# Modulation items of 1024 columns, and a projection that starts on the lower half of the features

## The chip, the core and the metric

One core of a Trainium2 chip runs the whole program. The metric is the device time of one execution in microseconds, as the median of several runs. TensorE (PE) does the matrix products, VectorE (DVE) and ScalarE (ACT) the elementwise work, GpSimd (POOL) and SyncE (SP) mostly issue DMAs; every engine works through its own instructions in order and is held back by semaphores. Numbers are fp32. A weight tile is therefore split into a high part (`whi`) and a low part (`wlo`), and a product is made of three matmuls: high by high, high by low, low by high.

## The reference

Two blocks of two layers each, for 256 tokens of width 1024. Only the first block is touched. Each of its four sub-layers is a "sandwich" that is modulated by a vector `c`:

```
def modulation(c, w, b):
    return jnp.split(jax.nn.silu(c) @ w + b, 3, axis=-1)

def sandwich(x, mod, g_pre, g_post, fn):
    shift, scale, gate = mod
    h = rms_norm(x, g_pre) * (1.0 + scale[:, None]) + shift[:, None]
    return x + gate[:, None] * rms_norm(fn(h), g_post)
```

`w` is a matrix of 1024 rows and 3072 columns (12 MB), one for each sub-layer: shift, scale and gate, 1024 columns each. The sub-layers are: 0, a hybrid mixer (`h @ hyb_w_in`, then pooling over windows and a gated recurrence, then `@ hyb_w_out`); 1, a feed-forward; 2, a dilated attention (`h @ att_w_qkv`); 3, a feed-forward.

## The kernel before

**Modulation.** `silu(c) @ w` is a product of one row with a big matrix. VectorE computes it as sums over the 8 groups of 128 rows: an *item* multiplies a tile of 128 rows by 512 columns with a column of `sc` (silu(c)) and adds it to an accumulator `acc_a` (or `acc_b`). TensorE then adds up the 128 partitions with a matmul against ones. Sub-layer 0 needs its shift and scale first of all: 4 column blocks x 8 items, loaded as 8 loads of 1 MB each into the six slots of `raw`, the buffer that the weights use too (`load`, line 378; `ada_first`, line 1325). Five of the 32 items are done by TensorE directly on the loaded rows (`DIRECT`, line 335; `ada_cols`, line 2512). `add_cols` (line 2499) does the sums and `mod_cols` (line 1346) makes the shift and scale columns from them, at its end `scol` at line 1351. Only then can the features of the normed x be shifted and scaled (`pre`, line 647 on ScalarE and 1507 on VectorE).

All other modulation (gate of sub-layer 0, then sub-layers 1 to 3) goes through `ada_ring`, two slots of 1 MB, each with 4 tiles of 128 x 512. GpSimd issues a load when VectorE has finished the 4 items of the slot (`ada_blocks`, line 455; semaphore `ada_step`). The items (`ada_item`, line 1302) are woven by hand into VectorE's order: behind the first blocks of the projection, into the eight levels of the recurrence, into the first feed-forward, and behind each block of four splits in the qkv projection (line 1799).

**Start.** SyncE loads the first four modulation loads, then x, four more, and then the projection's weights, two loads per column block (features 0 to 511 and 512 to 1023). ScalarE copies small tables, squares x for the norm, makes `xn1`, and after the modulation columns walks over the 8 feature groups: shifted h as fp32 and as high part, with the first weight splits between them. Then it issues the loads of `masks`, `bandqk` (pooling bands) and `poolw` (lines 809 to 811). TensorE turns x, does the column sums with `warm_ones` between them, and then projects block after block (`proj`, line 2254): all four half tiles of block 0 (kind A: tokens on partitions, matmuls of 512), then all four of block 1 (kind B, matmuls of 256). Behind them it waits for all three tables (`band_in`, line 2547) and multiplies the bands, then block 2, and then eight half blocks with the scores of one level of the recurrence after each (`level_scores`, line 2558), which wait for VectorE's `level` and `merge` (lines 1735 and 1724). VectorE's product at line 1719 starts the levels.

A split needs its tile of `raw`, and its slot among four in `whi`/`wlo` to be free: the high part by ScalarE (line 542), then the low one by VectorE (line 1299).

Of the kernel before, what the change touches and what calls it, by code (L numbers as in the profile page):

```python
# [24 lines left out]
P = 128  # L25
# [63 lines left out]
def program(nc, t):  # L89

    with ExitStack() as ctx:
# [27 lines left out]
        with ExitStack() as first:  # L119
            ada_ring = sb(first, "ada_ring", [P, 2, 4, 512])  # L120
# [165 lines left out]

        def slot(n):

            return (n + ADA_FIRST) % RAW

        def in_count(n):

            return 16 * ((n + ADA_FIRST) // RAW + 1)
# [41 lines left out]
        DIRECT = {6: (3,), 7: (2, 3)}  # L335
        DVE_LAST, PE_LAST = (4, 5), (6, 7)
# [40 lines left out]
        def _(sp):  # L377
            def load(n, it, src):
# [4 lines left out]
                if n >= RAW:  # L383
                    sp.wait_ge(s["lo_ready"], 2 * (n - RAW) + 2 + 12 * it)
                elif n + ADA_FIRST >= RAW:
                    sp.wait_ge(s["ada_used"], n + ADA_FIRST - RAW + 1)
                    if n + ADA_FIRST - RAW in DIRECT:
                        sp.wait_ge(s["ada_pe"], n + ADA_FIRST - RAW - 5)
                dst = raw[:, slot(n), :].rearrange("p (k n) -> p k n", k=k)
                sp.dma_start(dst, ap).then_inc(raw_in[slot(n)], 16)  # L390
# [63 lines left out]
        def _(pool):  # L454
            def ada_blocks(first, blocks):

                for i, (j, n) in enumerate(blocks):
                    b = first + i
                    for kh in range(2):
                        if b:  # L460
                            pool.wait_ge(s["ada_step"], 8 * (b - 1) + 4 * (kh + 1))
                        src, _ = src_cols(t["ada_w"][j // 2, j % 2], n, kh)
                        pool.dma_start(ada_ring[:, kh, :, :], src).then_inc(ada_in[kh], 16)  # L463
# [21 lines left out]
            SHIFT_SCALE, GATE = [0, 512, 1024, 1536], [2048, 2560]  # L485
            pool.wait_ge(s["ada_used"], ADA_FIRST)
            ada_blocks(0, [(0, n) for n in GATE])
            gain_row(0)
            ada_blocks(2, [(1, n) for n in SHIFT_SCALE])
            ada_blocks(6, [(1, GATE[0])])  # L490
            gain_row(1)
            ada_blocks(7, [(1, GATE[1])] + [(2, n) for n in SHIFT_SCALE + GATE])
# [5 lines left out]
            ada_blocks(14, [(3, SHIFT_SCALE[0])])  # L498
            gain_row(3)
            ada_blocks(15, [(3, n) for n in SHIFT_SCALE[1:] + GATE])  # L500
# [29 lines left out]
        def _(act):  # L530
# [116 lines left out]
            def pre(j):  # L647

                if j < 4:
                    act.wait_ge(s["mod_ready"], j + 1)  # L650
                for k in range(KD):
                    if j < 4 and k % 2:
                        act.wait_ge(s["h32_ready"], 4 * j + k // 2 + 1)
# [129 lines left out]

            for g in range(3):
                act.wait_ge(s["vec_dil"], g + 1)
                A.activation(vrow[:, g * VLEN_DIL:(g + 1) * VLEN_DIL], ps[0:8, 4 + g, 0:VLEN_DIL], ACT.Copy,
                             scale=1.0 / DIL_SCALE).then_inc(s["vec_dil_c"], 1)
            act.wait_ge(s["vec_dil"], 4)
            A.copy(vrow[:, 3 * VLEN_DIL:], ps[0:8, 7, :]).then_inc(s["vec_dil_c"], 1)
# [5 lines left out]
            norms(0)  # L795
            act.wait_ge(s["root_x"], 1)
            act.wait_ge(s["ssq_x"], 2)
            A.activation(xn1[:, 0, :], x[:, 0, :], ACT.Copy, scale=small[:, 5, 3:4]).then_inc(s["xn_ready"], 1)
            act.wait_ge(s["const_in"], 48)
            act.wait_ge(s["root_x"], 2)  # L800
            A.activation(diag[:, :], ident[:, :], ACT.Copy, scale=small[:, 5, 4:5]).then_inc(s["diag_ready"], 1)
            split(0)
            pre(0)
# [9 lines left out]
            for b in range(3):  # L813
                proj("hyb_in", HYB[b:b + 1], f1, tok1, b)
# [468 lines left out]
        def _(dve):  # L1283
# [18 lines left out]
            def ada_item(acc, b, n, k, it=0, bias=None):  # L1302

                kh, kk = k // 4, k % 4
                if kk == 0:
                    dve.wait_ge(ada_in[kh], 16 * (b + 1) + 32 * it)
                out = acc[:, bass.ds(n, 512)]
                if k == 0 and bias is not None:
                    dve.wait_ge(s[f"wrow_in{bias}"], 16)
                    ins = V.scalar_tensor_tensor(out=out, in0=ada_ring[:, kh, kk, :], scalar=sc[:, k:k + 1],  # L1310
                                                 in1=gg[:, bias, n:n + 512], op0=ALU.mult, op1=ALU.add)
                elif k == 0:
                    ins = V.tensor_scalar(out, ada_ring[:, kh, kk, :], sc[:, k:k + 1], None, ALU.mult)
                else:
                    dve.wait_ge(s["ada_step"], 8 * b + k + 16 * it)
                    ins = V.scalar_tensor_tensor(out=out, in0=ada_ring[:, kh, kk, :], scalar=sc[:, k:k + 1],  # L1316
                                                 in1=out, op0=ALU.mult, op1=ALU.add)
                ins.then_inc(s["ada_step"], 1)

            def ada_part(acc, b, n, kh, it=0, bias=None):  # L1320
# [1871 lines left out]
```

## Time and profile before

| what | us |
|---|---|
| median of 3 runs | 1269.61 (1267.96 to 1271.66) |
| the profiled execution | 1269.97 |
| its span | 1268.2 |
| TensorE, busy | 1248.5 |
| VectorE, busy | 933.9 |
| ScalarE, busy | 718.2 |

The profile is one execution. Its page names the busy time of each engine, the chain of work that ended last, and the costliest groups of instructions. From the trace come the chain in order of time, the instructions of an engine in a stretch, who waited for whom, the DMA issues with their time to landing, and stretches with the granted TensorE clock. A matmul that is written once in fp32 without a split shows as two. Matmul ends are modelled, so the busy share of TensorE says little; waits before an instruction and the distance between starts say more.

### The profile page before, as it was taken

The page shows a single profiled execution, that of the slowest core. Times are in us where ns is not written, and L with a number is a line of the kernel's source. Part 1 is how long each engine was busy: PE and PEld are TensorE (multiplying, and loading weights), DVE is VectorE, ACT ScalarE, POOL GpSimd, SP SyncE. Part 2 cuts the span into 40 slices and gives each one's busy share as a digit, 9 for nine tenths or more (in the row PEclk, how much of TensorE's full clock was granted, in tenths as well). Part 3 has the DMA queues.
Part 4 walks back from the last instruction along what each step waited for, and adds up shares of the span by engine and source line. Part 5 has one row for each costly group of instructions (what it writes and reads, how often), then busy time and mean ns, then how long its engine had stood idle before and what let it go on. Part 6 is the DMA issues. An engine that isn't in the chain of part 4 may idle for free.

```text
span 1268.2 us, 20841 instructions
## 1 busy us (share of the span) xinstructions
PE 1248.5 (98%) x8024; PEld 1133.6 (89%) x8024; DVE 933.9 (74%) x1222; ACT 718.2 (57%) x1069; POOL 50.8 (4%) x76
## 2 busy tenths in 40 slices
PE   8999999999999999999999999999999999999999
PEld 6998899999999778999989989888888888888888
DVE  6889988886899658666676695676666677666665
ACT  3676754444744557444467764665555667655554
POOL 1101000000111000000001000000000000000000
PEclk8999999999999999999999999999999999999999
DMA  9986989996799734666556544356565542366650
GB/s 348 372 297 208 339 290 325 334 327 205 244 361 370 230 67 153 206 203 200 199 166 211 162 150 155 132 198 200 200 202 202 190 163 95 122 220 204 202 166 34
DMA packets 147248, 274.41 MB, mean 216 GB/s; under 512 B 4759, under 2 KB 85679, under 8 KB 147048
## 3 DMA queue, kind: packets, MB, share of 16 engines
q1 hardware_dynamic: 132320, 220.21, 51.5%
q0 software_dynamic: 13616, 50.94, 11.9%
q10 hardware_dynamic: 1240, 2.26, 0.5%
q8 instruction: 49, 0.80, 0.3%
q14 instruction: 23, 0.19, 0.0%
HBM read 272.30 MB, written 1.10 MB: 216 GB/s over the span
## 4 chain that ended last, share of the span: by engine, by line
PE 82%; DVE 8%; DMA 4%; ACT 3%; issue 2%; ACTq 0%; POOL 0%; DVEq 0%; POOLq 0%
PE ps L2229 80%; DMA ada_ring<-in_ada_w 4%; DVE wlo L1299 2%; DVE acc_a L1316 2%; ACT whi L542 1%; PE ps L2682 1%; DMA voh<-in_voh 1%; ACT xn L603 0%; PE ps L2416 0%; PE ps L2399 0%; DVE rs L1949 0%; ACT h L659 0%; DVE prob L1906 0%; ACT hboth L654 0%; PE ps L2976 0%
## 5 line engine op out<-in xcount | busy, mean ns | idle before, releaser
L1299 DVE TENSOR_TENSOR wlo<-raw,whi 128x1024 fp32r<-128x1024 f32 x400 | 483.5, 1222 | 222.8 <-ACT whi L542 222.0
L542 ACT CAST whi<-raw 128x1024 fp32r<-128x1024 f32 x400 | 416.6, 1048 | 404.0 <-PE ps L2229 389.6
L2229 PE MATMUL ps<-hboth,whi 128*128 128x256 f32 (+1 forms) x2720 | 605.2, 311 | 1.0 <-DVE hboth L1529 0.5
L2229 PE MATMUL ps<-hboth,wlo 128*128 128x256 f32 x1792 | 491.6, 274 | 0.7 <-DVE hboth L1524 0.4
L2229 PEld LDWEIGHTS ps<-hboth,whi 128*128 128x128 f32 x2720 | 447.2, 191 | 30.1 <-issue 6.2
L2229 PEld LDWEIGHTS ps<-hboth,wlo 128*128 128x128 f32 x1792 | 343.9, 192 | 3.1 <-issue 0.6
L2229 PE MATMUL ps<-whi,hidhi 128*128 128x512 f32 x434 | 164.5, 379 | 0.0
L2229 PE MATMUL ps<-wlo,hidhi 128*128 128x512 f32 x434 | 164.1, 378 | 0.0
L2229 PE MATMUL ps<-whi,hidlo 128*128 128x512 f32 x434 | 164.1, 378 | 0.0
L2229 PE MATMUL ps<-whi,hboth 128*128 128x512 f32 (+1 forms) x512 | 155.8, 375 | 3.0 <-DVE wlo L1299 0.9
L2229 PEld LDWEIGHTS ps<-whi,hboth 128*128 128x128 f32 x512 | 95.5, 190 | 18.5 <-issue 5.1
L1316 DVE SCALAR_TENSOR_TENSOR acc_a<-ada_ring,sc,acc_a 128x512 f32<-128x512 f32 (+1 forms) x124 | 93.1, 751 | 7.6 <-DMA ada_ring<-in_ada_w 3.7
L2229 PE MATMUL ps<-wlo,hboth 128*128 128x512 f32 (+1 forms) x256 | 93.8, 366 | 0.0
L2229 PEld LDWEIGHTS ps<-whi,hidlo 128*128 128x128 f32 x434 | 82.0, 189 | 11.5
L2229 PEld LDWEIGHTS ps<-wlo,hidhi 128*128 128x128 f32 x434 | 82.1, 189 | 11.4 <-issue 0.2
L2229 PEld LDWEIGHTS ps<-whi,hidhi 128*128 128x128 f32 x434 | 82.2, 189 | 10.5 <-ACT whi L542 0.2
L2229 PEld LDWEIGHTS ps<-wlo,hboth 128*128 128x128 f32 x256 | 48.7, 190 | 6.2 <-issue 1.0
L463 POOL DMA_DIRECT2D ada_ring<-in_ada_w x40 | 30.0, 751 | 296.0 <-DVE acc_a L1316 212.6
L1651 DVE TENSOR_REDUCE tmp<-ps 128x512 f32<-128x1024 f32 x32 | 38.9, 1217 | 3.5 <-PE ps L2229 3.5
L1656 DVE TENSOR_TENSOR hidlo<-hid,hidhi 128x512 fp32r<-128x512 f32 x32 | 22.1, 692 | 16.6 <-ACT hidhi L760 16.6
L603 ACT ACTIVATE xn<-x 128x512 f32<-128x512 f32 (+1 forms) x32 | 19.3, 602 | 10.7 <-DVE x L1418 5.7
L755 ACT ACTIVATE tmp<-tmp 128x512 f32<-128x512 f32 x32 | 20.1, 627 | 2.9 <-DVE tmp L1651 2.9
(259 smaller groups left out, 1118.6 us busy)
## 6 DMA issues: line engine op xcount, KB each, us to landing
raw<-in_ffn_w_in SPq DMA_DIRECT2D x44, 1024.0 KB, 7.2
ada_ring<-in_ada_w POOLq DMA_DIRECT2D x40, 1024.0 KB, 7.9
raw<-in_w_mlp_up SPq DMA_DIRECT2D x32, 1024.0 KB, 5.4
raw<-in_w_mlp_down SPq DMA_DIRECT2D x32, 1024.0 KB, 4.9
raw<-in_ffn_w_out SPq DMA_DIRECT2D x22, 1024.0 KB, 5.1
raw<-in_att_w_qkv SPq DMA_DIRECT2D x18, 1024.0 KB, 7.3
raw<-in_w_in_even SPq DMA_DIRECT2D x18, 1024.0 KB, 5.1
raw<-in_hyb_w_in SPq DMA_DIRECT2D x10, 1024.0 KB, 11.2
```

The lines of the kernel that those rows point to most:

```text
L463: pool.dma_start(ada_ring[:, kh, :, :], src).then_inc(ada_in[kh], 16)
L542: A.copy(whi[:, H % 4, :], raw[:, slot(n), h * HALF:(h + 1) * HALF]).then_inc(s["hi_ready"], 1)
L603: A.activation(xn_of(j)[0][:, i // 2, c], x[:, i // 2, c], ACT.Square, accum_out=stat[:, 4 + i:5 + i]).then_inc(s["ssq_x"], 1)
L755: A.activation(tmp2[:, g % 3, :], tmp2[:, g % 3, :], ACT.Relu).then_inc(s["mrelu"], 1)
L1299: V.tensor_tensor(wlo[:, H % 4, :], raw[:, slot(n), h * HALF:(h + 1) * HALF], whi[:, H % 4, :].bitcast(F32), ALU.subtract).then_inc(s["lo_ ...
L1316: ins = V.scalar_tensor_tensor(out=out, in0=ada_ring[:, kh, kk, :], scalar=sc[:, k:k + 1], in1=out, op0=ALU.mult, op1=ALU.add)
L1651: V.tensor_reduce(in_order(tmp2[:, g % 3, :], 2), parts_of(UP_BANK[g % 3]), AX, ALU.add) \
L1656: V.tensor_tensor(hidlo2[:, g % 3, :], hid2[:, g % 3, :], hidhi2[:, g % 3, :].bitcast(F32), ALU.subtract).then_inc(s["mhid_lo"], 1)
L2229: return pe.matmul(out, lhsT, rhs, start=first, stop=last, skip_group_check=True)
L2682: m = pe.transpose(dl_turned(p, i)[:, (j - j0) * P:(j - j0 + 1) * P], dl_block(p, j), ident[:, :])
```

## The change

1. Ring items are 1024 columns wide: `ada_ring` holds 2 slots of 2 tiles of 128 x 1024. A load brings 256 rows of one part (shift, scale or gate) and is freed after two items. Bytes and multiplications are the same, items half as many. In the scale of sub-layer 1, TensorE's direct share becomes one group of rows (7) of 1024 columns instead of two of 512.
2. The order of the weaving follows: one wide item in each of the levels 1 to 7, two per stretch in the feed-forward, and in the qkv stage one item behind each split.
3. Sub-layer 0's first shift and scale: the loads come in the order lower half of shift, lower half of scale, upper half of shift, upper half of scale (`ADA_COLUMNS`); x is the second load; the lower weight halves of blocks 0 and 1 are loaded before the upper modulation loads. `first_mod(half)` makes the columns of 4 feature groups at a time. Two more items go to TensorE (`DIRECT`, load 3).
4. TensorE runs the lower halves of both blocks (q 0 to 3), then the sums for the upper features, then the upper halves (q 4 to 7). x is turned by transposes of both token tiles. The warming matmuls are 32 at the start, 12 and 8 later, and none between the halves. ScalarE does the first norm before it copies the tables of the bias, and issues the band tables behind the work of the upper features.

```diff
-            ada_ring = sb(first, "ada_ring", [P, 2, 4, 512])
+            ada_ring = sb(first, "ada_ring", [P, 2, 2, D])
...
-        DIRECT = {6: (3,), 7: (2, 3)}
-        DVE_LAST, PE_LAST = (4, 5), (6, 7)
+        ADA_COLUMNS = (0, 1024, 512, 1536)
+        DIRECT = {3: (2, 3), 6: (3,), 7: (2, 3)}
+        PE_LAST = 7
...
-            for a in range(ADA_FIRST):
-                load(a - ADA_FIRST, 0, src_cols(t["ada_w"][0, 0], (a // 2) * 512, a % 2))
-                if a == 3:
-                    sp.dma_start(x[:, :, :], t["x"][0].rearrange("(t p) n -> p t n", p=P)).then_inc(s["x_in"], 16)
-            proj(FIRST["hyb_in"], t["hyb_w_in"][0], HYB)
+            load_ada(0)
+            sp.dma_start(x[:, :, :], t["x"][0].rearrange("(t p) n -> p t n", p=P)).then_inc(s["x_in"], 16)
+            for a in range(1, 4):
+                load_ada(a)
+            for n in range(2):
+                load(n, 0, src_cols(t["hyb_w_in"][0], HYB[n][1], 0))
+            for a in range(4, ADA_FIRST):
+                load_ada(a)
+            for n in range(2, 4):
+                load(n, 0, src_cols(t["hyb_w_in"][0], HYB[n - 2][1], 1))
+            proj(FIRST["hyb_in"] + 4, t["hyb_w_in"][0], HYB[2:])
...
-            def ada_blocks(first, blocks):
...
+            def ada_loads(first, rows):
+
+                for i, (j, n, q) in enumerate(rows):
+                    l = first + i
+                    if l >= 2:
+                        pool.wait_ge(s["ada_step"], 2 * (l - 1))
+                    src, _ = src_down(t["ada_w"][j // 2, j % 2][:, n:n + D], 2 * P * q)
+                    pool.dma_start(ada_ring[:, l % 2, :, :], src).then_inc(ada_in[l % 2], 16)
...
+            act.wait_ge(s["turned"], 8)
+            for half in range(2):
+                split(4 * half)
+                act.wait_ge(s["mod_ready"], half + 1)
+                first_pre((4 * half, 4 * half + 1))
+                split(4 * half + 1)
+                first_pre((4 * half + 2, 4 * half + 3))
+                split(4 * half + 2)
+                split(4 * half + 3)
...
-            for a in range(4):
-                ada_first(a)
+            ada_first(0)
             mean_x(0, 0)
             mean_x(0, 1)
-            for a in range(4, ADA_FIRST):
+            for a in range(1, 4):
                 ada_first(a)
-            mod_cols(0, 0)
+            first_mod(0)
             split(0)
-            pre(0)
+            first_low(0)
+            first_low(1)
+            split(1)
+            first_low(2)
+            ada_first(4, (0,))
+            first_low(3)
+            split(2)
+            ada_first(4, (1, 2, 3))
+            split(3)
+            for a in range(5, ADA_FIRST):
+                ada_first(a)
+            first_mod(1)
+            split(4)
...
-                for q in range(i, i + 1) if i < 6 else range(3 * i - 12, 3 * i - 9):
-                    b, k = (q + 20) // 8, (q + 20) % 8
-                    ada_item(acc_a, b, 512 * b, k)
...
+                if 1 <= i <= 6:
+                    ada_item(acc_a, 1, D, i + 1)
...
             for b in range(8):
-                proj("qkv", (QKV_B * 2 + QKV_A)[b:b + 1], b)
-                if b < 6:
-                    ada_block(acc_a, 14 + b, 512 * b)
+                for q in range(4):
+                    split(2 * (FIRST["qkv"] + 2 * b) + 4 + q)
+                    if b < 6:
+                        ada_item(acc_a, 7 + b // 2, D * (b // 2), 4 * (b % 2) + q)
...
-            proj("hyb_in", HYB[0:2], j=0)
+            for q in range(8):
+                b = q // 2 % 2
+                proj_half(HYB[b][0], 2 * b, q, 2 * (q // 4) + q % 2, 0, None if b else 0)
+                if q == 3:
+                    add_cols(2)
+                    ada_cols(6)
+                    ada_cols(7)
+                    add_cols(3)
             pe.wait_ge(s["proj_free"], 1)
             pe.wait_ge(s["band_in"], 48)
```

## Rows read from the trace of the kernel before

**Rows 1.** The page's engine table: busy us, share, instructions.
```profile
PE 1248.5 (98%) x8024; PEld 1133.6 (89%) x8024; DVE 933.9 (74%) x1222; ACT 718.2 (57%) x1069; POOL 50.8 (4%) x76
```
**Rows 2.** The chain that ended last, by time: start us, us, what.
```profile
67.61 8.65 DMA ada_ring<-in_ada_w
...
81.33 1.22 DVE bandqk L1719
...
156.98 175.93 PE ps L2229 x1310
```
**Rows 3.** Waits of TensorE, 38 to 116 us: total, times, longest.
```profile
PE ps L2229 <- issue: 0.8, 1, 0.8
```
**Rows 4.** VectorE's instructions by time: start us, us, what, idle before.
```profile
11.12 3.11 DVE L1335 SCALAR_TENSOR_TENSOR acc_a<-raw,sc,acc_a 128x512 f32<-128x512 f32 x4 [1.92 <-DMA raw<-in_ada_w]
...
21.72 0.15 DVE L1394 TENSOR_SCALAR small<-stat 128x1 f32<-128x1 f32 x1 [1.27 <-ACT xn L603]
...
28.43 3.17 DVE L1335 SCALAR_TENSOR_TENSOR acc_a<-raw,sc,acc_a 128x512 f32<-128x512 f32 x4
...
35.84 0.17 DVE L1351 SCALAR_TENSOR_TENSOR scol<-scol,cols 128x8 f32<-128x8 f32 x1
36.04 1.22 DVE L1299 TENSOR_TENSOR wlo<-raw,whi 128x1024 fp32r<-128x1024 f32 x1
...
37.63 0.41 DVE L1524 TENSOR_TENSOR hboth<-h,hboth 128x256 fp32r<-128x256 f32 x1
```
**Rows 5.** ScalarE's instructions by time; ACTq are its DMA issues.
```profile
19.03 0.63 ACT L603 ACTIVATE xn<-x 128x512 f32<-128x512 f32 x1 [2.80 <-DMA x<-in_x]
...
39.01 0.56 ACT L659 ACTIVATE h<-ps,shcol,scol 128x256 f32<-128x256 f32 x1
...
43.45 0.36 ACTq L809 DMA_DIRECT2D masks<-in_masks  x1
...
44.82 0.46 ACTq L811 DMA_DIRECT2D poolw<-in_pool_w  x1
```
**Rows 6.** Stretches: length, busy us by engine, granted clock, DMA share, GB/s.
```profile
18.00:19.00 1.00, 1.00 (x8) 1.00 (x7) 0.96 (x2) 0.00 (x0) 0.00 (x0) 0.69 1.03 385
...
36.00:37.00 1.00, 1.00 (x6) 1.00 (x6) 0.97 (x2) 0.96 (x2) 0.00 (x0) 0.50 1.09 408
...
30.00:40.00 10.00, 10.00 (x71) 9.80 (x72) 5.57 (x11) 4.32 (x8) 1.54 (x2) 0.83 1.05 388
```
**Rows 7.** DMA issues, 43 to 45.5 us: KB each, us to landing.
```profile
bandqk<-in_band ACTq DMA_DIRECT2D x1, 1024.0 KB, 8.5
...
masks<-in_masks ACTq DMA_DIRECT2D x1, 512.0 KB, 4.5
poolw<-in_pool_w ACTq DMA_DIRECT2D x1, 256.0 KB, 11.3
```
**Rows 8.** TensorE's instructions by time.
```profile
9.91 5.71 PE L2229 MATMUL ps<-voh,vtab 33*8 33x384 f32 x8 [3.99 <-DMA voh<-in_voh]
...
34.50 0.95 PE L2229 MATMUL ps<-ones,acc_a 128*128 128x1 f32 x8
...
38.39 0.77 PE L2229 MATMUL ps<-whi,hboth 128*128 128x512 f32 x1
...
59.90 3.62 PE L2229 MATMUL ps<-bandqk,tok 128*128 128x256 f32 x16
```
**Rows 9.** VectorE in the levels of the recurrence, by time.
```profile
88.89 0.73 DVE L1316 SCALAR_TENSOR_TENSOR acc_a<-ada_ring,sc,acc_a 128x512 f32<-128x512 f32 x1
89.55 0.77 DVE L1747 TENSOR_TENSOR bandqk<-pooled,tot 128x512 f32<-128x512 f32 x1
...
113.31 0.16 DVE L1749 TENSOR_TENSOR tot<-f 128x8 f32<-128x8 f32 x1
```
**Rows 10.** Waits of ScalarE, 160 to 330 us; its copy in the qkv stage.
```profile
ACT whi L542 <- PE ps L2229: 86.5, 61, 1.6
...
402.08 1.01 ACT L550 COPY f<-ps 128x1024 f32 x1
```

More of the change, by code:

```diff
@@ L793, in _, with first_pre @@
             act.dma_start(t["vec_swa"], vrow[:, 3 * VLEN_DIL:]).then_inc(s["vec_out"], 16)
[L795 to L802, printed above, removed]
-            pre(0)
+            def first_pre(parts):
+                for k in parts:
+                    if k >= 4:
+                        act.wait_ge(s["hlo_ready"], k - 3)
+                    A.activation(h32_slot(0, k), turned_ps(0, k), ACT.Identity, bias=shcol[:, 0, k:k + 1],
+                                 scale=scol[:, 0, k:k + 1])
+                    A.activation(hhi[:, k, :], turned_ps(0, k), ACT.Identity, bias=shcol[:, 0, k:k + 1],
+                                 scale=scol[:, 0, k:k + 1]).then_inc(s["hhi_ready"], 1)
+            act.wait_ge(s["turned"], 8)
[7 more added lines that the diff above has]
+                split(4 * half + 3)
             act.wait_ge(s["lb_step"], 1)
@@ L813, in _ @@
             for b in range(3):
-                proj("hyb_in", HYB[b:b + 1], f1, tok1, b)
+                if b == 0:
+                    split(8)
+                    split(9)
+                    evac(0, 6, "A", HYB[0][2], f1, tok1)
+                elif b == 1:
+                    split(10)
+                    split(11)
+                    evac(1, 8, "B", HYB[1][2], f1, tok1)
+                else:
+                    proj("hyb_in", HYB[b:b + 1], f1, tok1, b)
                 if b == 1:
@@ L1308, in ada_item @@
                 if k == 0 and bias is not None:
                     dve.wait_ge(s[f"wrow_in{bias}"], 16)
[L1310 to L1311 removed]
+                    ins = V.scalar_tensor_tensor(out=out, in0=row, scalar=sc[:, k:k + 1], in1=gg[:, bias, :],
+                                                 op0=ALU.mult, op1=ALU.add)
@@ L1318, in ada_item, with ada_items @@
+                    ins = V.scalar_tensor_tensor(out=out, in0=row, scalar=sc[:, k:k + 1], in1=out, op0=ALU.mult,
+                                                 op1=ALU.add)
                 ins.then_inc(s["ada_step"], 1)
-            def ada_part(acc, b, n, kh, it=0, bias=None):
-                for kk in range(4):
-                    ada_item(acc, b, n, 4 * kh + kk, it, bias)
-            def ada_first(a):
-                dve.wait_ge(raw_in[a % RAW], 16 * (a // RAW + 1))
+            def ada_items(acc, w, n, ks, it=0, bias=None):
+                for k in ks:
+                    ada_item(acc, w, n, k, it, bias)
@@ L1328, in ada_first @@
+            def ada_first(a, parts=range(4)):
+                at = ada_ring_at(a)
+                dve.wait_ge(raw_in[at % RAW], 16 * (at // RAW + 1))
                 mine = [kk for kk in range(4) if kk not in ada_direct(a)]
-                for kk in mine:
-                    k, w = 4 * (a % 2) + kk, raw[:, a % RAW, kk * 512:(kk + 1) * 512]
+                for kk in [kk for kk in mine if kk in parts]:
+                    k, w = 4 * (a % 2) + kk, raw[:, at % RAW, kk * 512:(kk + 1) * 512]
                     out = acc_a[:, (a // 2) * 512:(a // 2 + 1) * 512]
@@ L1353, in mod_cols, with first_mod, first_low @@
                     .then_inc(s["mod_ready"], 1)
-                dve.wait_ge(s["mod_ready"], j + 1)
+                dve.wait_ge(s["mod_ready"], j + 2)
+            def first_mod(half):
+                k, bank = 4 * half, 4 * half
+                dve.wait_ge(s["cols_sum"], 2 * half + 2)
+                V.tensor_tensor(shcol[:, 0, k:k + 4], ps[:, bank, 0:4], col("b_shift", k, 4), ALU.add)
+                link(V.tensor_tensor(scol[:, 0, k:k + 4], ps[:, bank, 4:8], col("b_scale", k, 4), ALU.add))
+                V.scalar_tensor_tensor(out=scol[:, 0, k:k + 4], in0=scol[:, 0, k:k + 4], scalar=1.0,
+                                       in1=col("g_pre", k, 4), op0=ALU.add, op1=ALU.mult) \
+                    .then_inc(s["mod_ready"], 1)
+            def first_low(k):
+                dve.wait_ge(s["hhi_ready"], k + 1)
+                V.tensor_tensor(hlo[:, k, :], h32_slot(0, k), hhi[:, k, :].bitcast(F32), ALU.subtract) \
+                    .then_inc(s["hlo_ready"], 1)
             def gate_add(j, bank):
```

192 lines of the change are left out of this document (106 added, 86 removed).

## The prediction

> **What bounds the kernel now.** I read the page's engine table first, then the chain of waits from its start, then the waits of TensorE, and only then single stretches. TensorE is busy for 98% of the span [rows 1], so there is little to win except where it starts late or waits. The chain says where that is. Until 49 us it runs through TensorE only in name: from 26 to 38 us the engine does sums of a few columns and warming matmuls, and the first matmul of the projection is at 38.39 [rows 8]. Between 50 and 93 us the chain is not TensorE's: it goes through the modulation items on VectorE and the loads of their ring (8.65 us for one) up to the product at L1719 [rows 2]. Yet TensorE itself waits hardly at all there: after 38.4 us its longest wait is 0.8 us, at 112.7 [rows 3]. So two legs run side by side from 38 to 113 us within one microsecond of each other: TensorE's matmuls, and VectorE with its ring. Whoever shortens one gets only what the other allows. From 157 us the chain is TensorE alone for 176 us at a stretch [rows 2].
>
> The first 38 us have three limits. DMA moves 388 GB/s or so without a pause [rows 6], 2.7 us for a load of 1.05 MB. VectorE needs 0.785 us for each item (3.17 us for four, with the wait between them) and ends its last one at 31.6; the modulation columns are done at 36.04 [rows 4]. TensorE can't start before them.
>
> **Early phase, lower features.** x is moved from fifth to second load. The first load lands at 6.3 as before; x takes the place of the second, which VectorE used at 11.12, so x is there at 11.1. VectorE's second mean comes 2.7 us after ScalarE's first square (19.03 and 21.72, [rows 4, 5]), so at 13.9, and the weights of load 1, now third, are there at that time too. Load 1: 3.15 us, load 2: 2.85, two items of load 3: 1.6; VectorE is at 21.5. TensorE turns x and takes two rows of load 3 itself; its column sums take 1 us (0.95, [rows 8]) and the three small operations 0.5: lower columns at about 23.2. Their two halves of each block run from about 25 to 36.5.
>
> **Upper features.** After 23.2 VectorE has 4 weight splits (1.14 apart, 4.6), 4 low parts (0.4 each, 1.6 [rows 4]), 13 items (9.9) and about 1.5 us of waits for ScalarE: 40.8. Sums and columns again 1.5: the upper columns are ready at 42.3, against 36.0 now for all of them. That is the price of the split order: the same column work, with 4 splits and 4 low parts now ahead of it. ScalarE is the queue for what follows (for each feature row two shifted copies, 0.56 long and 0.46 apart [rows 5], and a split of 0.95 for every second). First upper matmul at 43.9. The eight half blocks take 59.90 - 38.39 = 21.5 us [rows 8], so four take 10.75: 54.7. I add 0.5 for ScalarE and 1.0 for the clock: 56.2, against 59.9. The matmuls of the lower halves lie under VectorE's 13 items, so they cost nothing; if they ran late the upper ones would follow them.
>
> The clock: between the lower and the upper halves the new TensorE order holds column sums and waits, and the warming matmuls are gone. In the trace the granted clock fell to 0.50 at 36 us after such columns although the engine counted as busy, and in the other place, after 4 us without matmuls (5.9 to 9.9), it came back to 1.00 only within the microsecond from 18 to 19 [rows 6, 8]. So the upper halves will start at the lower of the two levels (1.2 GHz); from the first place, about 3 us of it, half lost and part of that beside ScalarE, 1.0 us; from the second, 8.8 us of it, 4.4 us. The Trainium skill (TensorE: Matmul & The Clock Gate, "Why this matters for your kernels") advises against gaps between bursts of matmuls, which speaks against this order; by it TensorE would be ready at 59.6 at worst, and the trace agrees that the engine falls back.
>
> **The tables behind it.** The wait that I expect to be last is a hidden one. After these blocks TensorE multiplies the pooling bands at 59.90 and needs masks, bands and pool weights. ScalarE issues them in program order behind the copies of the last features: at 43.45 to 44.82, 7.4 us after the columns, and they landed at 56.1, 12.7 us from the first issue (masks 4.5, bands 8.5, pool weights 11.3) [rows 5, 7]. That left 3.8 us of slack. In the new order ScalarE has all copies and splits of the upper half ahead of them; with the same three instructions of lead over the engine I get 4.3 us after the columns: 46.6. Landing: if the queue got an even half of 385 GB/s, its 1.84 MB take 9.6 us (56.2); as in the trace 12.7 (59.3); and up to 3.1 us more (62.4) when the third ring load, issued near 53.9 now, shares with the pool weights, which are short rows. I take 60.3, nearest to the trace, plus 1 for the ring load. So TensorE, ready at 56.2, multiplies the bands at 60.3: 0.4 later than now. The cover that made ScalarE's place free is gone.
>
> **TensorE's leg.** From the bands to the end of the level scores it goes from 59.90 to 112.7, of which 0.8 was waiting [rows 2, 3]: 111.9 if nothing is late, plus 0.4: 112.3.
>
> **VectorE's leg.** An item of 1024 columns isn't in the trace. Below: a split of the same size, 1.22 us, 1.14 apart [rows 4]; above: two items of 512, 1.57 chained or 1.32 among other work (0.66 each, 88.89 to 89.55 [rows 9]). I take 1.3 chained and 1.2 among other work, near the split, since both read two inputs of 1024. Up to the product 20 old items (15.7) become 10 (13.0): 2.7 less. They start at 51.2 instead of 51.60. Ring loads carry the same bytes and are freed after two items as after four before. The product can't come before ScalarE's and TensorE's part, though: bands at 60.3, copy at 64, eight small operations, four splits, evacuation and Silu near 78. I get its end at 79.3 by ScalarE and at 80.9 by the ring, 80.1 in the middle, instead of 82.5 (81.33 + 1.22, [rows 2]). Then the levels: six single items (0.66, one of them cheaper) and three more at 109.81 (2.3), 6.0 in all, become six items of 1.2, 7.2 in all. So 31.0 us from the product to the last level step (113.3 to 113.5 [rows 9]) become 32.2. Leg: 80.1 + 32.2 = 112.3, against 113.5. The item that stood ahead of the low part (L1764) is gone (0.66), but TensorE waits for ScalarE's copy beside it, so I count nothing.
>
> **Afterwards.** From 115.5 to 148 TensorE has no wait, and its column sums hold as many matmuls as before (8 direct ones on one row of 1024 instead of two of 512). In the first feed-forward ScalarE waits for TensorE 61 times, 86.5 us [rows 10]: VectorE's savings there are worth nothing. In the qkv stage the blocks follow at 10.72 us, and only the one evacuated at 402.08 [rows 10] came 0.34 later than that, since splits stood behind eight items and a ring load. Interleaved, a ring slot needs two items, a split and a load (3.6, and 8 as for the loads of the start), 11.6 us against 10.72, about 4 us over five blocks, but each split now has some 6 us of room and no longer four splits behind eight items. I count 0.3 gained; the loss of that cover would cost up to 4.
>
> **Sum.** Legs 112.3 against 113.5: 1.2, and 0.3: 1.5 us. Profiled execution 1269.97 (span 1268.2 and 1.8 around it) - 1.5 = 1268.5; it stands 0.4 above the median of 1269.61.
>
> **Rivals.** (B) The tables are in time (56.2) and the product at 78: TensorE's leg 108.2, VectorE's 110.2, gain 3.3 + 0.3: 1266.4; with upper columns at 40.5 instead of 42.3, some 5.5: 1264.5. For it: the DMA may have idle room near 45 us, as loads wait for slots then. Against: ScalarE's order, and VectorE's levels, which get longer. (C) Slower: the tables, at the bands' matmul. It decides from 61.5 on, where TensorE's leg passes 113.5; at 63.5 it costs 2.0 less 0.3: 1271.7, and only past 65.3 more than 0.3%. The slow clock (59.6) delays the ring's freeing and adds to it. (D) The wide items save nothing (1.32 among other work, 1.57 chained): product 2.7 later, 82.8, levels 0.7 more: leg 115.7, 1271.9. (E) The change doesn't do what it says in the qkv stage: the ring falls behind, splits are late, up to 3 us: 1271.5.
>
> **How the numbers follow.** Forecast 0.50, B 0.27, C 0.13, D 0.05, E 0.05. About 0.3% (3.8 us) is what a measurement can tell from no change. More than that is reached by the far part of B (0.18) and by the far part of C with D or E on top (0.10); within it: 0.72. Range: 1264.3 takes in B's far end, 1272.4 takes in C at 64.
>
> **What would show it.** Upper columns (L1351's successor) at 42.3 and the first upper matmul at 43.9; a wait of TensorE of about 4 us for the pool weights ahead of the band matmul; items of 1024 at 1.28 us busy; the last level step at 112.3; the first feed-forward unchanged in length. Wrong would be: no wait at the bands, level steps paced by TensorE, or a gap in qkv.

## The result and the profile after

The changed kernel is slower by 0.17%: 1272.55 us against 1270.16, medians of 20 runs each, a ratio of 1.0017 with the interval 1.0009 to 1.0025. Its profiled execution has a span of 1271.4 us against 1268.2. TensorE is as busy as before and VectorE 20 us less [rows 1]; the page's first line of busy times:

```profile
PE 1249.7 (98%) x8012; PEld 1137.8 (89%) x8012; DVE 913.8 (72%) x1140; ACT 721.5 (57%) x1073; POOL 48.9 (4%) x76
```

So the loss isn't work, it is waiting. The chain that ended last, by time (start us, us, what), says where; it answers to [rows 2]:

```profile
65.73 8.99 DMA ada_ring<-in_ada_w
...
113.74 32.65 PE ps L2318 x178
...
155.02 175.93 PE ps L2318 x1310
...
376.97 7.97 DMA ada_ring<-in_ada_w
384.94 0.02 issue
384.96 1.28 DVE acc_a L1374
386.25 1.14 DVE wlo L1357
387.38 1.21 DVE acc_a L1374
388.59 0.29 issue
388.88 9.55 DMA ada_ring<-in_ada_w
398.43 0.02 issue
398.45 1.28 DVE acc_a L1374
```

The long piece of the first feed-forward starts at 155.02 instead of 156.98 and is as long as before, 175.93. Up to 332 us the changed kernel is 1.96 us ahead in this pair of profiles (how far single profiles can be trusted for that is said in the last section). Then, from 352 to 401, the chain no longer holds TensorE at all: it goes round through an item of the ring, a split, the slot's second item, the issue and the next load. ScalarE's copies close the blocks; of before (two lines, the second one is the last copy of the stage) and of after (three):

```profile
391.02 1.01 ACT L550 COPY f<-ps 128x1024 f32 x1
...
437.46 1.01 ACT L552 COPY tok<-ps 128x1024 f32<-128x1024 f32 x1
```
```profile
391.44 1.01 ACT L584 COPY f<-ps 128x1024 f32 x1
406.47 1.01 ACT L584 COPY f<-ps 128x1024 f32 x1
...
440.68 1.01 ACT L586 COPY tok<-ps 128x1024 f32<-128x1024 f32 x1
```

These blocks are 10.72 us apart when nothing is late. After's copies at 391.44 and 406.47 are 15.0 apart; before's at 391.02 and 402.08 [rows 10] 11.1. The lead of 1.96 has turned into a lag of 3.2 at 440, and nothing changes behind that. The 50 us from 350 to 400 (length, busy us by engine, granted clock, DMA share, GB/s), before and then after:

```profile
350.00:400.00 50.00, 49.89 (x447) 49.73 (x446) 46.99 (x56) 23.44 (x23) 7.03 (x10) 1.00 1.02 372
```
```profile
350.00:400.00 50.00, 46.57 (x413) 46.06 (x412) 36.73 (x33) 22.53 (x22) 5.62 (x8) 1.00 0.98 349
```

One number is useful for all that follows: from the start of the long feed-forward piece to the last of these copies it is 437.46 - 156.98 = 280.48 us before and 440.68 - 155.02 = 285.66 after. I call it the stretch F. The time from the start of the program to that piece I call S.

### The profile page after: what moved, and what is told of

Same layout as the page of the kernel before. It is cut to its first block, busy times and chain, and to the rows that moved or that the text cites. A ratio compares the mean times of both kernels' runs of the same rounds, so it can differ in the third digit from the quotient of the medians.

```text
span 1271.4 us, 20717 instructions
## 1 busy us (share of the span) xinstructions
PE 1249.7 (98%) x8012; PEld 1137.8 (89%) x8012; DVE 913.8 (72%) x1140; ACT 721.5 (57%) x1073; POOL 48.9 (4%) x76
## 4 chain that ended last, share of the span: by engine, by line
PE 80%; DVE 8%; DMA 5%; ACT 4%; issue 3%; ACTq 0%; SPq 0%; DVEq 0%
PE ps L2318 78%; DMA ada_ring<-in_ada_w 4%; DVE wlo L1357 2%; DVE acc_a L1374 2%; ACT whi L576 1%; DMA x<-in_x 1%; PE ps L2780 1%; ACT xn L637 1%; PE ps L2505 0%; DVE rs L2038 0%; ACT h L693 0%; DVE prob L1995 0%; DVE acc_a L1394 0%; PE ps L2488 0%; ACT hboth L688 0%
## 5 line engine op out<-in xcount | busy, mean ns | idle before, releaser
L2318 PEld LDWEIGHTS ps<-wlo,hidhi 128*128 128x128 f32 x434 | 82.3, 190 | 11.3 <-issue 0.2
L2318 PEld LDWEIGHTS ps<-whi,hidlo 128*128 128x128 f32 x434 | 82.3, 190 | 11.3
L1374 DVE SCALAR_TENSOR_TENSOR acc_a<-ada_ring,sc,acc_a 128x1024 f32<-128x1024 f32 (+1 forms) x62 | 79.5, 1282 | 14.0 <-DMA ada_ring<-in_ada_w 13.1
```

Source lines behind the costliest of these rows:

```text
L1374: ins = V.scalar_tensor_tensor(out=out, in0=row, scalar=sc[:, k:k + 1], in1=out, op0=ALU.mult, op1=ALU.add)
L2318: return pe.matmul(out, lhsT, rhs, start=first, stop=last, skip_group_check=True)
```

## The experiments

**Order or width in the qkv stage.** Two things are new there: an item stands behind each split, and items are twice as wide. Four kernels take these apart, and the start with them. The first is the changed kernel with its items grouped as before:

```diff
             for b in range(8):
-                for q in range(4):
-                    split(2 * (FIRST["qkv"] + 2 * b) + 4 + q)
-                    if b < 6:
-                        ada_item(acc_a, 7 + b // 2, D * (b // 2), 4 * (b % 2) + q)
+                proj("qkv", (QKV_B * 2 + QKV_A)[b:b + 1], b)
+                if b < 6:
+                    for q in range(4):
+                        ada_item(acc_a, 7 + b // 2, D * (b // 2), 4 * (b % 2) + q)
```

> The changed kernel, with its four wide items of a qkv block behind the block's four splits again instead of one behind each split. Theory S (how long a ring slot is held): interleaved, the two items of a slot have a split between them, so a slot is held 3.6 us and then needs a load of 8 to 9.5 us, 11.6 to 13.1 against a block of 10.72; grouped it is held 2.6 us, so 10.6 plus. The ring keeps up, the 1.96 us won before the qkv stage stay, the copy that is at 406.47 in the changed kernel is at 400 to 401, and the time is 1270.2 - 2.0 = 1268.2 (1267.7 to 1268.9). Rival W (the load itself became slower because its rows are 1024 columns long, 8 to 9.5 us instead of 7.3 to 8.3): the ring stays late in either order, 1270.5 to 1272.5.

Measured: 1265.89 us, 0.9965 of before (0.9952 to 0.9977), 6.7 less than the changed kernel; it is the fastest of all. Rival W falls. F is 278.97 us. The forecast of 1268.2 was too high by 2.3, because I took before to be free of this loss; it isn't (run e8_before_light). VectorE's order in one block, by time:

```profile
357.10 2.60 DVE L1374 SCALAR_TENSOR_TENSOR acc_a<-ada_ring,sc,acc_a 128x1024 f32<-128x1024 f32 x2
360.67 2.60 DVE L1374 SCALAR_TENSOR_TENSOR acc_a<-ada_ring,sc,acc_a 128x1024 f32<-128x1024 f32 x2 [0.97 <-DMA ada_ring<-in_ada_w]
363.19 4.62 DVE L1357 TENSOR_TENSOR wlo<-raw,whi 128x1024 fp32r<-128x1024 f32 x4
```

And its stretch from 350 to 400:

```profile
350.00:400.00 50.00, 50.00 (x439) 49.68 (x438) 43.72 (x38) 23.81 (x24) 7.83 (x11) 1.00 1.03 392
```

VectorE still waits for the ring (0.97), but it does so when the block's splits are done, and TensorE has no gap in 50 us.

The second is the kernel before with narrow items interleaved:

```diff
             for b in range(8):
-                proj("qkv", (QKV_B * 2 + QKV_A)[b:b + 1], b)
-                if b < 6:
-                    ada_block(acc_a, 14 + b, 512 * b)
+                for q in range(4):
+                    split(2 * (FIRST["qkv"] + 2 * b) + 4 + q)
+                    if b < 6:
+                        ada_item(acc_a, 14 + b, 512 * b, 2 * q)
+                        ada_item(acc_a, 14 + b, 512 * b, 2 * q + 1)
```

> The kernel before, with its items of 512 columns, but in the qkv stage two of them behind each split instead of eight behind the four splits. Theory S: a slot's four items have a split in their middle, so it is held 4 x 0.785 + 1.14 = 4.3 us and with a load of 8 its cycle is 12.3 us against 10.72: as in the changed kernel VectorE waits for the ring with splits behind the wait, and about 5 us are lost in the qkv stage: 1273 to 1276. Rival W (width is the cause): no loss, 1270.2 within 0.5.

Measured: 1276.00 us, 1.0046 of before (1.0029 to 1.0063), as theory S has it. F is 286.81. The order costs about as much with narrow items: 6.2 us by the medians, but against a kernel that loses some itself (run e8_before_light); against an F without loss, 278.96, it is 7.9 here and 6.7 with wide items.

The third weaves the wide items in pairs:

```diff
                 for q in range(4):
                     split(2 * (FIRST["qkv"] + 2 * b) + 4 + q)
-                    if b < 6:
-                        ada_item(acc_a, 7 + b // 2, D * (b // 2), 4 * (b % 2) + q)
+                    if b < 6 and q % 2:
+                        ada_items(acc_a, 7 + b // 2, D * (b // 2), (4 * (b % 2) + q - 1, 4 * (b % 2) + q))
```

> The changed kernel with its qkv items woven in another way: two items behind every second split instead of one behind each. Two splits still stand behind each pair of items, but the two items of a ring slot are next to each other, so a slot is held 2.6 us as with grouped items, not 3.6. Theory S (the time a slot is held counts): the cycle is 2.6 + 8 = 10.6 us, the ring keeps up: 1265.9 (1265.4 to 1266.9). Rival O (splits that stand behind an item's wait for a load are what costs, however long a slot is held): half of the 6.7 us and more stays: 1269 to 1272.5.

Measured: 1266.48 us, 0.9970 of before (0.9960 to 0.9980). F is 279.09. The 6 us are gone, although two splits still stand behind each pair, and rival O falls. The loads are no faster; us to landing of the ring's ten loads from 345 to 405 us (min, median, max), in the changed kernel and then in this one:

```profile
DMA to landing us min/median/max: 7.1/8.4/9.6
```
```profile
DMA to landing us min/median/max: 6.8/8.4/9.5
```

So what costs is the split between the two items of one slot: it makes the slot be held longer.

The fourth leaves the order alone and takes away bytes:

```diff
+                    width = D // 2 if l >= 30 else D
-                    src, _ = src_down(t["ada_w"][j // 2, j % 2][:, n:n + D], 2 * P * q)
-                    pool.dma_start(ada_ring[:, l % 2, :, :], src).then_inc(ada_in[l % 2], 16)
+                    src, _ = src_down(t["ada_w"][j // 2, j % 2][:, n:n + width], 2 * P * q)
+                    pool.dma_start(ada_ring[:, l % 2, :, 0:width], src).then_inc(ada_in[l % 2], 16)
```

> The changed kernel, interleaved in the qkv stage as it is, but the last ten ring loads bring only 512 of their 1024 columns (the other half of an item multiplies what lay in the slot, so the shift, scale and gate of sub-layer 3 are not computed). All instructions, waits and orders stay. Theory S (a slot's load arrives after its item is due): with half the bytes a load takes 4 to 5 us instead of 8 to 9.5, the cycle is 8 to 9 us against 10.72, the gap vanishes: 1265.9, as with grouped items. Rival O (the order itself delays the splits, since VectorE has an item ahead of each): no or little change, 1271 to 1272.5.

Measured: 1266.27 us, 0.9975 of before (0.9966 to 0.9985). F is 278.96. Rival O falls here too. A load of half the bytes still took 6.7 us to land, not the 4 to 5 that I gave it, against 8.4 in the changed kernel; 1.7 us less per load was enough. (The weights' loads got more room as well, so this run alone would not prove the held slot; the pairs above, with all bytes, do.)

**The start and the width, each alone.** The start alone, with the items, the loads of the ring and all later orders of before:

```diff
-            ada_ring = sb(first, "ada_ring", [P, 2, 2, D])
+            ada_ring = sb(first, "ada_ring", [P, 2, 4, 512])
...
-            ada_items(acc_a, 0, 0, range(4), 0, 0)
+            ada_block(acc_a, 0, 0, 0)
             proj("hyb_in", HYB[1:2], 1)
-            ada_items(acc_a, 0, 0, range(4, 8))
+            ada_block(acc_a, 1, 512, 0)
```

> The kernel before with the new start alone (loads of the lower columns first, lower halves of two blocks ahead of the upper columns, ScalarE's new order), ring items of 512 columns and all later orders as before. Theory of two legs: TensorE reaches the bands 1.8 us earlier (58.1 instead of 59.90), but VectorE's items and their ring still end at about 82 before the product and 113.1 at the last level step, so only about 0.4 us reach the end: 1269.8 (1269.2 to 1270.3). Rival P (TensorE's start alone decides): the whole 1.8: 1268.4.

Measured: 1269.83 us, 0.9999 of before (0.9989 to 1.0008). F is 281.96, 1.5 us worse than before's. The forecast was met in its number only, and this run alone can't tell whether a gain at the start was lost again. The two runs with light loads, below, take that up.

The wide items alone, with the start of before and grouped in the qkv stage:

```diff
-            ada_ring = sb(first, "ada_ring", [P, 2, 4, 512])
+            ada_ring = sb(first, "ada_ring", [P, 2, 2, D])
...
-                    ada_block(acc_a, 14 + b, 512 * b)
+                    for q in range(4):
+                        ada_item(acc_a, 7 + b // 2, D * (b // 2), 4 * (b % 2) + q)
```

> The kernel before with ring items of 1024 columns alone, grouped behind the splits in the qkv stage, and the old start. Theory of two legs: VectorE's ten wide items ahead of the product take 2.7 us less, but TensorE's own work from the bands (59.90) to the end of the level scores held only 0.8 to 1.6 us of waits, so the end of the levels comes 0.5 to 1.2 earlier: 1269.0 to 1269.7. Rival V (VectorE's leg alone decides): 1.8 earlier as in the changed kernel: 1268.4.

Measured: 1267.42 us, 0.9979 of before (0.9969 to 0.9989), with F at 278.96, 1.5 shorter than before's. Against before it hit neither number, since the qkv part of the gain was in neither theory.

So both sides need a qkv stage that can't lose. The kernel before and the start alone, with half the bytes in the last ring loads (the same edit for both):

```diff
+                        width = 256 if b >= 15 else 512
-                        pool.dma_start(ada_ring[:, kh, :, :], src).then_inc(ada_in[kh], 16)
+                        pool.dma_start(ada_ring[:, kh, :, 0:width], src[:, :, 0:width]).then_inc(ada_in[kh], 16)
```

> The kernel before with its last ten ring loads reduced to half their bytes (shift, scale and gate of sub-layer 3 not computed), the rest unchanged. In its qkv stage one block came 0.34 us late and one 1.18 us late. Theory S: both are the ring's, so 1.5 us vanish: 1268.3 (1267.5 to 1268.9). Rival: they are of another cause, no change: 1269.8.

> The new start alone on ring items of 512 columns (run e3_start_only), with the last ten ring loads reduced to half their bytes (shift, scale and gate of sub-layer 3 not computed), so that the qkv stage can lose nothing to the ring. Against run e8_before_light it shows what the start alone is worth. Theory of two legs: VectorE's narrow items and their ring hold the levels, 0.4 us less than e8_before_light (0 to 0.7). Rival P: the start's own 1.5 to 1.8 us, which in run e3_start_only were lost again in the qkv stage.

Measured: 1267.04 us (0.9981; 0.9972 to 0.9990) for before and 1268.27 (0.9990; 0.9982 to 0.9999) for the start alone; F is 278.96 in both. The kernel before thus loses 1.5 us to the ring in its profile, and some 2.5 by the medians (1269.52 in that series, 1267.04); the forecast of 1267.5 to 1268.9, made from the profile, was too high. The start alone, which rival P put 1.5 to 1.8 us ahead and my theory 0.4, gains nothing; it came out 1.2 behind. Four kernels without a loss in the qkv stage (F 278.96 or 278.97), medians:

| | start of before | new start |
|---|---|---|
| items of 512 | 1267.04 | 1268.27 |
| items of 1024 | 1267.42 | 1265.89 |

Each part alone is worth nothing or less; the two together are worth 1.15 us. Only the rows were measured in one series each: there the new start is 1.2 slower with narrow items and 1.5 faster with wide ones. The 1.15 goes across series; with each kernel against its own before it is 1.5 (3.9 less against 2.5 less), and it is not much more than the noise. That the start pays only with wide items fits two legs of nearly the same length. The columns mix two ways to spare the qkv stage, but run e6_half_bytes, wide items and new start with light loads, is at 1266.27, so that the way matters little. Whether the start costs anything without wide items isn't settled: the two legs don't explain it, the intervals of the upper two overlap, the run times of one kernel spread by 1 to 4 us, and in their profiles the last level step is at the same time. First the band matmul on TensorE and that step on VectorE before (light):

```profile
60.02 3.62 PE L2230 MATMUL ps<-bandqk,tok 128*128 128x256 f32 x16
...
112.75 0.16 DVE L1750 TENSOR_TENSOR tot<-f 128x8 f32<-128x8 f32 x1
```

and with the new start alone (light):

```profile
57.77 3.69 PE L2318 MATMUL ps<-bandqk,tok 128*128 128x256 f32 x16 [1.14 <-DMA poolw<-in_pool_w]
...
112.72 0.16 DVE L1838 TENSOR_TENSOR tot<-f 128x8 f32<-128x8 f32 x1
```

TensorE reaches the bands 2.25 us earlier, and 55 us later the levels end where they did, as they would if VectorE with its narrow items held them. Two single profiles don't show more than that: in e2_narrow_inter, the same program as before up to there, the bands are at 58.27 and the last step at 111.04, and in e3_start_only at 57.54 and 111.53. What stands is the medians: with narrow items the new start was not faster in either series.

**Which leg decides in the new kernel.** Warming matmuls between the lower and upper halves, some ahead of the last column sums:

```diff
                     ada_cols(6)
+                    for _ in range(2):
+                        mm(ps[:, 5, 0:P], ones[:, :], ones[:, :])
                     ada_cols(7)
+                    for _ in range(2):
+                        mm(ps[:, 5, 0:P], ones[:, :], ones[:, :])
                     add_cols(3)
+                    for _ in range(5):
+                        mm(ps[:, 5, 0:P], ones[:, :], ones[:, :])
```

> The changed kernel with grouped items in the qkv stage (run e1_wide_grouped, 1265.9 us) and nine 128 x 128 matmuls against ones between the lower and the upper halves, in a bank whose features have been read: two behind each of the sums on loaded rows, five behind the last column sums. In the changed kernel the granted clock was 0.50 from 39.0 to 49.2 us; the column sums behind 37.6 took 5.9 us instead of 3.8, and seven of the upper matmuls ran at half speed, 1.7 us. Theory of two legs: TensorE's leg gets 2.5 us shorter, VectorE's only the 1.0 us by which the upper columns (43.85) come earlier, since ScalarE's copies and VectorE's splits follow them: 1264.9 (1264.3 to 1265.5). Rival P (TensorE's leg alone decides): 1263.4. Rival V (VectorE with its ring alone, whose first loads are long there): 1265.9.

Measured: 1267.37 us (0.9982; 0.9972 to 0.9992), 1.5 more than e1_wide_grouped. All three theories came out too low; mine had let the columns come 1.0 earlier. The clock didn't hold (0.98 in the microsecond to 40, 0.50 after it), so the sums ran behind the warming ones at half speed. Its windows there, and then the columns and the bands:

```profile
39.00:40.00 1.00, 1.00 (x11) 1.00 (x11) 0.83 (x2) 0.02 (x1) 0.00 (x0) 0.98 1.05 385
40.00:41.00 1.00, 1.00 (x6) 1.00 (x7) 0.00 (x0) 0.00 (x0) 0.84 (x2) 0.50 1.04 383
```
```profile
43.66 0.16 DVE L1418 SCALAR_TENSOR_TENSOR scol<-scol,cols 128x4 f32<-128x4 f32 x1
...
56.82 3.62 PE L2318 MATMUL ps<-bandqk,tok 128*128 128x256 f32 x16
```

In e1_wide_grouped the columns were at 42.25 and the bands at 57.77. Here TensorE's leg is 0.95 shorter, VectorE's starts 1.41 later, and the end is 1.1 (spans 1264.5 and 1263.4) to 1.5 us later. The 95% intervals of the two runs overlap, so that it is later at all isn't sure; that nothing is gained from a shorter TensorE leg (rival P, 1263.4) is. Only the last five warming matmuls, none ahead of the sums:

```diff
                     add_cols(3)
+                    for _ in range(5):
+                        mm(ps[:, 5, 0:P], ones[:, :], ones[:, :])
```

> Run e1_wide_grouped (1265.9 us) with five 128 x 128 matmuls against ones behind the last column sums of the upper features and none ahead of them, so that the columns are not delayed (in run e5_grouped_warm they came 1.41 us later, 43.66 instead of 42.25, TensorE reached the bands 0.95 us earlier, and the time was 1.5 us longer). Theory V (VectorE's leg decides from the upper columns to the product; TensorE has room): the columns stay at 42.3 and the first ring item at 51.3, TensorE reaches the bands up to 1.7 us earlier, and nothing reaches the end: 1265.9 (1265.4 to 1266.4). Rival P (TensorE's leg decides): 1264.2 to 1264.9.

Measured: 1266.90 us (0.9975; 0.9967 to 0.9984); columns at 42.09, and no gain, as theory V has it, though 0.5 above its range. Why it is 1.0 above e1_wide_grouped isn't shown. The ring's loads let VectorE wait 5.0 us ahead of the product here and 2.2 there, but in the other kernels with this start it was 2.1 to 5.9 in single executions; and e11_wide_pairs, measured in the same series as this run, is only 0.4 below it. TensorE waited, too, for the last of the tables:

```profile
57.18 3.69 PE L2318 MATMUL ps<-bandqk,tok 128*128 128x256 f32 x16 [0.66 <-DMA poolw<-in_pool_w]
```

So its leg got only 0.6 us shorter, not 1.7, and this run is a weak test of which leg decides.

Last, the price of VectorE's items in the levels:

```diff
-                    ada_item(acc_a, 1, D, i + 1)
+                    ada_item(acc_a, 1, D, i + 1, wide=P)
```

> Run e1_wide_grouped with the six ring items in the levels of the recurrence cut to 128 of their 1024 columns (the shift of sub-layer 1 is not computed); all loads, waits and orders stay. It takes some 6 x 1.0 us from VectorE's leg behind the product. Theory of two legs: TensorE's and ScalarE's part of each level is close behind, so only 0.7 to 2.5 us reach the end: 1263.4 to 1265.2. Rival V (VectorE's levels alone decide): 6 us: 1259.9.

Measured: 1264.58 us (0.9956; 0.9942 to 0.9971). The six items take 0.35 us each instead of 1.30, 5.7 in all, and 1.3 reach the end by the medians, 1.9 by the spans (1261.5 against 1263.4). In e1_wide_grouped the chain that ended last still goes through five of the six items (the first line below is one); in this run it is TensorE alone for the whole of the levels (second line):

```profile
89.59 1.31 DVE acc_a L1374
```
```profile
77.81 31.90 PE ps L2318 x252
```

So with full items VectorE's leg decides, and TensorE is about 2 us behind it.

## Why the prediction was wrong

It gave 1268.5 (1264.3 to 1272.4), a gain of 1.5 us; measured are 1272.55, past the upper end, and a small but sure loss. The legs of the start came out near the forecast; the qkv term behind them, put at 0.3 us gained, was 5.2 lost. That the total still lies within 0.3% of before, as 0.72 of the chances had it, is luck: about 2 us won ahead of that stage set off part of the loss.

- **Lower features right, upper features late.** Lower columns 23.05 (forecast 23.2), first lower matmul 25.67 (25), lower halves done at 36.4 (36.5). The upper columns came at 43.69, forecast 42.3, though VectorE had ended its items at 40.3 (40.8): the term that was too small is the 1.5 for sums and columns. It took 3.4, since TensorE did the last sums at the lower clock, and VectorE waited 3.10 for them; in the other profiles with this start and no warming matmul ahead of the sums the columns came at 41.63 to 42.38. The clock fell between the halves as forecast, but its price for the upper halves was not 1.0: [rows 6] answer to the 0.51 and 0.50 here, and at 45.67 TensorE starts its upper halves at the lower level, until 49.2, some 1.75 us lost. The worse place of the two that I had priced (4.4 us, 59.6), to which I had tied the Trainium skill's advice against gaps (TensorE: Matmul & The Clock Gate, "Why this matters for your kernels"), was not reached. All in all the bands' matmul is at 58.06, forecast 56.2 for TensorE alone. (A window as above, then VectorE's first instruction on the upper columns, then TensorE's instructions.)

```profile
39.00:40.00 1.00, 1.00 (x7) 1.00 (x7) 0.96 (x2) 0.15 (x1) 0.00 (x0) 0.51 1.06 391
```
```profile
43.42 0.16 DVE L1416 TENSOR_TENSOR shcol<-ps,cols 128x4 f32<-128x4 f32 x1 [3.10 <-PE ps L2318]
```
```profile
37.62 3.98 PE L2318 MATMUL ps<-sc,raw 128*128 128x1 f32 x24
41.47 1.84 PE L2318 MATMUL ps<-ones,acc_a 128*128 128x1 f32 x8
45.67 0.76 PE L2318 MATMUL ps<-whi,hboth 128*128 128x512 f32 x1 [2.35 <-DVE hboth L1425]
...
58.06 3.62 PE L2318 MATMUL ps<-bandqk,tok 128*128 128x256 f32 x16
```

- **The tables: right that the slack is gone, wrong in size.** I took ScalarE to issue them three instructions ahead of its engine, at 46.6. They go out at 44.05 to 45.17, while ScalarE works on the first three of its eight copies (by time, start us, us; ACTq are its DMA issues):

```profile
43.89 0.56 ACT L839 ACTIVATE h<-ps,shcol,scol 128x256 f32<-128x256 f32 x1 [4.73 <-DVE scol L1418]
44.05 0.36 ACTq L858 DMA_DIRECT2D masks<-in_masks  x1
...
45.17 0.45 ACTq L860 DMA_DIRECT2D poolw<-in_pool_w  x1
```

  The pool weights need 11.7 us (11.3 in [rows 7]) and are there at 56.9, not at 60.3. No wait is left in the changed kernel, and 0.5 to 1.1 us in four of the experiments' profiles. The case of the Trainium skill's turns between queues (DMA: Bandwidth & Descriptors, "Queues, rings and completion order"), which I had put at 62.4, did not show. (Two small slips in rival C: by its own sum it passes 0.3% from 65.6 on, not 65.3, and comes to 1272.2 at 64, not 1272.4. They change nothing here.)
- **VectorE's leg: near the forecast.** An item takes 1.28 us (1.30 forecast), the product ends at 80.2 (80.1), and the last level step is at 111.67 (112.3); before, 113.31 [rows 9]. By these profiles the levels end 1.64 earlier, forecast 1.2; but kernels that are the same up to there end them at 110.39 to 111.67 with the changed code and at 111.04 to 113.31 with that of before, so that the hit is partly luck. The medians of the table above put the gain at 1.15 to 1.5.

```profile
79.01 1.22 DVE L1808 TENSOR_TENSOR bandqk<-f 128x1024 f32<-128x1024 f32 x1
...
111.67 0.15 DVE L1838 TENSOR_TENSOR tot<-f 128x8 f32<-128x8 f32 x1
```

- **The feed-forward: right.** 175.93 us before and after, and ScalarE waits 86.6 us in 61 waits for TensorE (86.5, 61 [rows 10]).
- **The qkv stage: the step that failed.** I had the mechanism in the text, with its sum (3.6 + 8 = 11.6 us against 10.72, about 4 us over five blocks), and set it off against "some 6 us of room" for each split, which made it a gain of 0.3. That is a slip of reasoning: room is used up once, while a ring that is too slow falls further behind with each block. Against before, F is 5.2 us longer; the sum had it 0.3 shorter. And the sum of one round was low. The chain shows 1.28 + 1.14 + 1.21 + 0.29 = 3.9 us held and loads of 7.97 to 9.55; from 352.15 to 388.88 three rounds took 12.2 each, 1.5 too long. By the medians the order costs 6.7 us against grouped items, where I had allowed 4 in the text and 3 in rival E. Rival E was what happened; I gave it 0.05. With the 4 of the text it would have come to 1269.97 - 1.2 + 4 = 1272.8, outside the range that I gave.
- **What I didn't see in before.** Its stage had lost time as well, 1.5 us by F (280.48 against 278.96) and some 2.5 by run e8_before_light: the chain in order of time shows it, as it goes through ring loads four times between 355 and 408. I read only the 0.34 at 402.08 and missed that the next but one copy, at 423.98, came another 1.2 late. A stage that already loses is no cover.

From before to after in measured steps: before 1270.2, less 2.8 (1269.82 to 1267.04, the ring's loss, gone with light loads and also with wide grouped items), less 1.15 (both legs), plus 6.7 (the split between a slot's two items): 1272.9, against 1272.55. These terms are differences between neighbouring medians, so that they close is bookkeeping and no proof; what shows the cause is the runs with grouped, paired and light loads.

**Why the room is so small** is seen in the bytes. Two weight loads and two ring loads per block are 4 x 1.05 MB in 10.72 us: 391 GB/s. In e1_wide_grouped the DMA moved 392 GB/s over 50 us at a share of 1.03, just what the blocks ask for, so there is hardly anything over to make up for a load that is issued late. After moved 349 and e2_narrow_inter 346, at shares of 0.98 and 0.95: there slots of the ring were held while the DMA moved some 45 GB/s less than in e1_wide_grouped. The Trainium skill (DMA: Bandwidth & Descriptors, "Bandwidth") names about 358 GB/s for a core whose neighbour on the same memory streams too, and has measured 425 for one alone. By 358 a block would take 11.7 us in any order; no run here had such a neighbour, and the 392 on this one core lies between the page's two figures.

## What to carry to other kernels

For a ring of few slots, add up one round: from the first use of a slot to its last, plus the issue, plus the load as it takes in that stage; if that is longer than the stage's period the deficit adds up with each round, and nothing that is parked between two uses of one slot is free. Weave at the grain of a slot, not of an item. Where two legs run side by side, an edit of one leg shows nothing, and one that is judged alone would be thrown away: measure the pair.

## What the runs showed of the hardware

- TensorE's granted clock fell from 1.00 to 0.50 between 39 and 41 us in the changed kernel and in e1, e5, e9 and e10, while the engine counted as fully busy: with matmuls of one column, and in e5_grouped_warm with four of 128 x 128 among them. It came back at 46.8 in e5 and between 47 and 48 in e9, both with warming matmuls behind the sums; without them between 47 and 48 in e10, at 49.2 in after, and not before 50 in e1. So the warming ones brought at most 3 us, and perhaps nothing. The Trainium skill (TensorE: Matmul & The Clock Gate, "HAM oscillation — how this bites in real kernels") explains the fall by gaps between bursts; here the clock fell ahead of the gap (TensorE had its 2.35 us of idle time only behind 43).
- Programs that are the same up to there differed by up to 2.25 us in S from one execution to another, and hardly at all behind it: with the start of before, S was 156.98, 154.73 and 156.56, while F was 278.96 or 278.97 in eight kernels. A gain of 1 to 2 us in the first 150 us can't be read from one profile of each; the 1.96 in the section on the result is such a number.
